# The relative bias of a hybrid decoder step on one core: read from 128 shifted copies in DRAM instead of turned with flip products

## The reference, cut to what matters

```python
b_own = rel_bias[_rel_bucket(q_pos[:, None] - own_pos[None, :])].astype(jnp.float32)
lo = lo + jnp.transpose(b_own, (0, 2, 1))[None]
causal = (own_pos[None, :] <= q_pos[:, None])[None, :, None, :]
lo = jnp.where(causal, lo, NEG)
```

## Time and profile before

| | us |
|---|---|
| median of 3 runs | 1690.98 (1690.12 to 1692.19) |
| the profiled execution's own time | 1688.32 |
| its span, first to last instruction | 1686.6 |
| TensorE busy | 1645.7 (98%) |
| VectorE busy | 1055.3 (63%) |
| ScalarE busy | 616.7 (37%) |
| GpSimd busy | 232.1 (14%) |
| mean granted TensorE clock | 0.992 of 2.4 GHz |

### The profile page before, as it was taken

The page is one execution under the profiler, slowest core; times in us unless marked ns, Lnnn a source line. Parts: engine busy times, 40 slices in busy tenths (PEclk is TensorE's granted clock), DMA queues, the critical chain, the costliest instruction groups (busy, mean ns, idle before and its releaser), DMA issues.

```text
span 1686.6 us, 30879 instructions
## 1 busy us (share of the span) xinstructions
PE 1645.7 (98%) x12884; PEld 1590.6 (94%) x12884; DVE 1055.3 (63%) x1702; ACT 616.7 (37%) x783; POOL 232.1 (14%) x371
## 2 busy tenths in 40 slices
PE   8999999999999999999999999999999999999996
PEld 7998889888898998999999999999999999999996
DVE  5676588455654355586766666666666666666665
ACT  6444323332233334463333333333333333333334
POOL 1112242023202011120101010101010101010004
PEclk9999999899999999999999999999999999999999
DMA  8433345344756565545454545454545454545442
GB/s 248 126 113 112 109 138 151 101 125 129 228 180 193 182 211 170 172 131 157 145 156 144 157 141 159 141 159 140 160 140 161 139 161 139 160 140 158 143 150 82
DMA packets 230171, 255.12 MB, mean 151 GB/s; under 512 B 9036, under 2 KB 220558, under 8 KB 229712
## 3 DMA queue, kind: packets, MB, share of 16 engines
q1 hardware_dynamic: 217488, 220.16, 42.6%
q0 software_dynamic: 9856, 31.71, 6.0%
q10 hardware_dynamic: 2688, 1.27, 0.3%
HBM read 242.00 MB, written 11.12 MB: 150 GB/s over the span
## 4 chain that ended last, share of the span: by engine, by line
PE 87%; DVE 4%; issue 3%; DMA 2%; POOL 2%; ACT 2%; POOLq 0%; DVEq 0%; SPq 0%; ACTq 0%
PE ps_proj L1693 21%; PE ps_proj L1694 20%; PE ps_proj L1695 20%; PE ps_small L1694 6%; PE ps_small L1693 6%; PE ps_small L1695 6%; PE ps_small L1730 2%; ACT w_hi L790 1%; DMA k_pages<-in_cache_k_dram 1%; DMA state_s<-in_state_gdn_dram 1%; DVE w_lo L1127 1%; DVE state_s L1122 1%; PE ps_small L1959 0%; PE ps_small L2070 0%; PE ps_small L1859 0%
## 5 line engine op out<-in xcount | busy, mean ns | idle before, releaser
L1693 PE MATMUL ps_proj<-x_hi,w_hi 128*128 128x320 f32 x2560 | 812.8, 317 | 3.6 <-issue 3.4
L1695 PE MATMUL ps_proj<-x_hi,w_lo 128*128 128x320 f32 x2560 | 794.8, 310 | 0.0
L1694 PE MATMUL ps_proj<-x_lo,w_hi 128*128 128x320 f32 x2560 | 794.8, 310 | 0.0
L1127 DVE TENSOR_TENSOR w_lo<-w_raw,w_hi 128x1024 fp32r<-128x1024 f32 x408 | 500.3, 1226 | 430.2 <-ACT w_hi L790 429.4
L790 ACT ACTIVATE w_hi<-w_raw 128x1024 fp32r<-128x1024 f32 x408 | 431.9, 1059 | 748.0 <-PE ps_proj L1695 551.1
L1693 PEld LDWEIGHTS ps_proj<-x_hi,w_hi 128*128 128x128 f32 x2560 | 483.8, 189 | 19.1 <-issue 15.6
L1694 PEld LDWEIGHTS ps_proj<-x_lo,w_hi 128*128 128x128 f32 x2560 | 484.5, 189 | 1.6 <-issue 1.6
L1695 PEld LDWEIGHTS ps_proj<-x_hi,w_lo 128*128 128x128 f32 x2560 | 484.0, 189 | 0.0
L1693 PE MATMUL ps_small<-hid_hi,w_hi 128*128 128x320 f32 x704 | 217.9, 309 | 0.0
L1695 PE MATMUL ps_small<-hid_hi,w_lo 128*128 128x320 f32 x704 | 217.6, 309 | 0.0
L1694 PE MATMUL ps_small<-hid_lo,w_hi 128*128 128x320 f32 x704 | 217.5, 309 | 0.0
(11 more groups left out here) (329 smaller groups left out, 1078.3 us busy)
## 6 DMA issues: line engine op xcount, KB each, us to landing
w_raw<-in_w_up_dram SPq DMA_DIRECT2D x176, 512.0 KB, 3.5
w_raw<-in_w_in_dram SPq DMA_DIRECT2D x112, 512.0 KB, 3.7
w_raw<-in_w_down_dram SPq DMA_DIRECT2D x88, 512.0 KB, 3.5
w_raw<-in_w_out_dram SPq DMA_DIRECT2D x32, 512.0 KB, 3.7
k_pages<-in_cache_k_dram POOLq DMA_DIRECT2D x32, 256.0 KB, 3.5
v_pages<-in_cache_v_dram POOLq DMA_DIRECT2D x32, 256.0 KB, 4.1
state_s<-in_state_gdn_dram POOLq DMA_DIRECT2D x10, 512.0 KB, 5.6
out_ss_dram<-state_s POOLq DMA_DIRECT2D x8, 512.0 KB, 4.4
```

The costliest lines, as they stand in the source:

```text
L1127: dve.tensor_tensor(wlo[:, slot], raw[:, slot], whi[:, slot].bitcast(F32), ALU.subtract).then_inc(lo_done, 1)
L1693: pe.matmul(o, hi, rhs_hi[:, k0 + kk_, :], start=first and kk_ == 0, stop=False)
L1694: pe.matmul(o, hi, rhs_lo[:, k0 + kk_, :], start=False, stop=False)
L1695: ins = pe.matmul(o, lo, rhs_hi[:, k0 + kk_, :], start=False, stop=last and kk_ == CQ - 1)
```

## The change

The bias row of each head is written 128 times, one behind the other, to a new tensor in DRAM, `rb_copies` (8 x 128 x 384, 1.57 MB), by one transfer from DRAM to DRAM that GpSimd issues in chunk 20. The bias tile is then read with a pitch of 383 entries where a copy is 384 long, so each partition's row begins one entry earlier than the one before: that is the shift in the direction that is wanted. The load goes straight to `bias_q`. The flip products, the copy out of PSUM and the constant `flip` are gone. Since the load now writes `bias_q`, it waits for the last readers of those bytes: in group 0 for `("P", "us", 1, 3)` and the output of the state that lies there, in group 1 for the last SS of group 0. `("G", "hk", 0)` moves from slot (71, 1) to (82, 0), behind the state outputs. The table `LENGTH` loses `hk` of TensorE and gets shorter numbers for the other two, by which the planner puts all steps of group 1 earlier.

```diff
@@ -52,7 +52,6 @@
         "ident": c == r,
-        "flip": c == P - 1 - r,
         "ones": np.ones((P, P)),
@@ -191,7 +190,7 @@
         if k == (1, 2):
-            s += [("P", "gs"), ("A", "gs"), ("G", "gs"), ("G", "hk", 0)]
+            s += [("P", "gs"), ("A", "gs"), ("G", "gs")]
         s += [("P", "kk", *k)]
@@ -254,8 +253,9 @@
 def att_steps(g):
-    s = ([("G", "hk", g)] if g else []) + [("G", "pk", g, 0), ("G", "pk", g, 1)]
-    s += [("P", "hk", g), ("V", "hk", g), ("P", "hb", g), ("V", "hb", g)]
+    s = [("G", "pk", g, 0), ("G", "pk", g, 1)] 
+    s = s + [("G", "hk", g)] if g else [("G", "hk", g)] + s
+    s += [("V", "hk", g), ("P", "hb", g), ("V", "hb", g)]
     for t in range(3):
@@ -301,12 +301,12 @@
           "os": 20, "ot": 6, "gs": 7,
-          "ks": 9, "us": 12, "sh": 11, "hk": 20, "kv": 12, "S": 11, "O": 12, "kt": 10, "hb": 6, "SS": 6, "PT": 4, "PV": 16, "OT": 2, "ab": 76},
+          "ks": 9, "us": 12, "sh": 11, "kv": 12, "S": 11, "O": 12, "kt": 10, "hb": 6, "SS": 6, "PT": 4, "PV": 16, "OT": 2, "ab": 76},
     "A": {"sc2": 25, "sc5": 24, "ab": 10, "qs": 10, "pl": 8, "o": 10, "oq": 0, "kv": 16, "E": 14, "SE": 9, "gs": 10, "kt": 8, "PT": 9, "fp": 22},
     "V": {"sc1": 11, "sc3": 50, "sc4": 15, "ss": 0, "gt": 0, "dm": 10, "dc": 0, "kk": 20, "kq": 9, "tk": 0, "bv": 0,
-          "o2": 0, "oz": 0, "dx": 10, "dh": 4, "df": 4, "dg": 6, "ks": 8, "st": 0, "oc": 10, "o1": 0, "um": 8, "us": 28, "hk": 40,
+          "o2": 0, "oz": 0, "dx": 10, "dh": 4, "df": 4, "dg": 6, "ks": 8, "st": 0, "oc": 10, "o1": 0, "um": 8, "us": 28, "hk": 8,
           "S": 16, "N": 9, "SS": 15, "SN": 7, "kt": 8, "hb": 12, "qz": 3},
-    "G": {"rn": 0, "or": 0, "so": 0, "si": 0, "s2": 0, "gs": 0, "zm": 0, "zv": 0, "kv": 0, "pk": 0, "pv": 0, "hk": 100, "mk": 9, "xd": 0, "qz": 0},
+    "G": {"rn": 0, "or": 0, "so": 0, "si": 0, "s2": 0, "gs": 0, "zm": 0, "zv": 0, "kv": 0, "pk": 0, "pv": 0, "hk": 0, "mk": 9, "xd": 0, "qz": 0},
 }
@@ -338,6 +338,7 @@
     slots[ROOT_AT, 1] += [("P", "root"), ("V", "root")]
+    slots[20, 0].append(("G", "rbcopy"))
     chain = [(x, ROOT_AT + 1) for x in scalar_steps()]
@@ -354,8 +355,6 @@
     def length(x):
-        if x == ("G", "hk", 0):
-            return 0
         return LENGTH[x[0]].get(x[1], 5) * PACE[x[0]] * SPREAD["attention" if x in attention else "delta"]
@@ -397,7 +396,7 @@
 SLOTS = schedule()
-TRANSFERS = {"si", "s2", "so", "gs", "hk", "kv", "pk", "pv"}
+TRANSFERS = {"rbcopy", "si", "s2", "so", "gs", "hk", "kv", "pk", "pv"}
 
@@ -544,7 +543,6 @@
     vp = a.put("v_pages", [P, 4, 2, 4, P])
-    hk = nc.alloc_sbuf_tensor_at("hankel", [P, 4, 2 * P], F32, offset=vp_at + 3 * 4096)
     ob = a.put("o_tok", [P, P])
@@ -569,6 +567,7 @@
     rb_dram = nc.dram_tensor("rb_scratch", (NH, 3 * P), F32, kind="Internal").ap()
+    rb_copies = nc.dram_tensor("rb_copies", (NH, P, 3 * P), F32, kind="Internal").ap()
     psA = nc.alloc_psum_tensor("ps_proj", [P, 4, 512], F32)
@@ -633,7 +632,7 @@
     ab_in, pt_in = sem("ab_in"), sem("page_table_in")
-    rb_out, hk_in, kv_out = sem("rb_out"), sem("hankel_in"), [sem(f"kv_out{i}") for i in range(2)]
+    rb_out, rb_copied, hk_in, kv_out = sem("rb_out"), sem("rb_copied"), sem("hankel_in"), [sem(f"kv_out{i}") for i in range(2)]
     pk_in = [sem(f"k_pages_in{i}") for i in range(2)]
@@ -1433,9 +1432,7 @@
                     g = k[0]
-                    after(dve, "P", "hk", g)
-                    dve.wait_ge(s_out[2], 32)
-                    chain(dve.tensor_copy(bm[:, :, :], psB[:, 2:4, :].rearrange("p k (h x) -> p (k h) x", h=2)))
+                    dve.wait_ge(hk_in, 16 * (g + 1))
                     finish(tt(bm[:, :, P:2 * P], bm[:, :, P:2 * P], over_heads(C("causal"), 4), ALU.add))
@@ -1977,14 +1974,6 @@
 
-                elif name == "hk":
-                    g = k[0]
-                    pe.wait_ge(hk_in, 16 * (g + 1))
-                    after(pe, *(("V", "oz", 1, 2) if g == 0 else ("A", "OT", 0, 1)))
-                    for i in range(2):
-                        ins = pe.matmul(psB[:, 2 + i, :], C("flip"), hk[:, 2 * i:2 * i + 2, :].rearrange("p h x -> p (h x)"),
-                                        start=True, stop=True)
-                    finish(ins)
                 elif name == "kv":
@@ -2021,6 +2010,7 @@
                     after(pe, "V", "hk", g)
+                    after(pe, *(("A", "OT", 0, 1) if g else ("V", "oz", 1, 2)))
                     for h in range(4):
@@ -2298,15 +2288,20 @@
                         pool.dma_start(gs_[r * P - rows_p:r * P - rows_p + n, :], gst[0:n, r, :]).then_inc(gs_out, 16)
+                elif name == "rbcopy":
+                    pool.wait_ge(rb_out, 16)
+                    pool.dma_start(rb_copies, rb_dram.unsqueeze(1).broadcast_to([NH, P, 3 * P])).then_inc(rb_copied, 16)
                 elif name == "hk":
...
                     if g == 0:
-                        pool.wait_ge(rb_out, 16)
-                        after(pool, "A", "gs")
+                        pool.wait_ge(rb_copied, 16)
+                        pool.wait_ge(s_out[2], 32)
+                        after(pool, "P", "us", 1, 3)
                     else:
-                        after(pool, "P", "PV", 0, 1)
-                    src = bass.AP(rb_dram.tensor, 4 * g * 3 * P, [[1, P], [3 * P, 4], [1, 2 * P]])
-                    pool.dma_start(hk[:, :, :], src).then_inc(hk_in, 16)
+                        after(pool, "P", "SS", 0, DB - 1)
+
+                    src = bass.AP(rb_copies.tensor, 4 * g * P * 3 * P + P - 1, [[3 * P - 1, P], [P * 3 * P, 4], [1, 2 * P]])
+                    pool.dma_start(bm[:, :, :], src).then_inc(hk_in, 16)
                 elif name == "kv":
@@ -2329,8 +2324,6 @@
                             after(pool, "P", "PV", *((g, 0) if b > 3 else (0, 1)))
-                        if b == 3:
-                            after(pool, "P", "hk", g)
                         cache, tile_, arrived = I["cache_v"], vp, pv_in
```

## The result

| | before | the change |
|---|---|---|
| median of 22 runs, us | 1689.16 (1684.27 to 1692.95) | 1692.03 (1689.77 to 1698.13) |
| ratio | | 1.0021, interval 1.0012 to 1.0031 |
| the profiled execution, us | 1688.32 | 1692.54 |
| its span, us | 1686.6 | 1690.8 |
| mean granted clock in it | 0.992 | 0.991 |

The change makes the kernel slower by 0.21%, 3.5 us, with an interval of 2.0 to 5.2 us. The ratio is not the quotient of the two medians, which differ by 2.9 us. The profiled executions differ by 4.2 us.

A forecast was written before the change was run, and what follows sets the result against it. TensorE, busy 98%, was taken to bound the kernel. Terms -3.4 + 2.8 + 2.9 + 1.6 + 0 = +3.9 us, added to the median 1690.98, gave 1694.9 us, slower by 0.23%; range 1690.4 to 1698.0.

The forecast's parts named there:

- Removed: Flip products of both groups on TensorE go, 1.71 us a group: -3.4 us.
- The gap of group 0: TensorE waits at `P hb`, near chunk 82, for VectorE's mask, which waits for the bias load: +2.8 us, 2.4 to 3.6.
- The gap of group 1: TensorE waits at `P hb`, chunk 113, for the mask, which follows `x_lo` on VectorE: +2.9 us, 2.7 to 3.1.
- The clock: TensorE's granted clock falls behind one of the two new gaps, one chance in two each: +1.6 us, 0 to 3.2.
- my rival of 1696.5 us: The clock falls behind both new gaps at `P hb`: +5.5 us in all, chance 0.15.
- What was put at nothing: Copy in chunk 20, later group 0 pages and V steps, group 1 running earlier: 0 us.
- The copy: GpSimd issues the 1.57 MB transfer in chunk 20, 0.89 us inside an idle time of 1.48 us: 0 us.
- The earlier place of group 1: Group 1 runs 4 to 5 chunks earlier with the same distances between steps: 0, within 1 us either way.
- The traffic: Rival: transfers in chunk 20 and around 550 make one weight chunk 3.5 us late: +7.4, 1698.4 us, chance 0.05.
- A missing gap: Rival: no wait at one `P hb` and no fall of the clock: -0.5, 1690.5 us, chance 0.08.
- The faster rival: Low-clock stretches before the changed steps run at full clock, giving back 5.8 us: -3.5, 1687.5 us, chance 0.07.
- the slow stretches of the linear part: Lower granted clock for 12 us from 320 and 4 us at 272, costing 4.6 and 1.2 us, 5.8 in all.

The follow-up runs named there:

- the kernel with the flips twice: The kernel before, with each pair of flip products issued twice into the same banks: ratio 1.0020, 1693.2 us.
- the versions without gaps: The change with planned lengths altered so that both `P hb` come later, group 1 three chunks early or all steps in old slots: 0.9974, again 0.9988; 0.9967.
- the old data path with the new table: The kernel before, keeping flip products, PSUM copy and small load, with only the planner's `hk` lengths as in the change: ratio 1.0025, 1692.5 us.
- both late: The change with `P hb` planned in a later slot in both groups, (83, 1) and (114, 2): ratio 0.9974, run again 0.9988.
- the copy alone: The kernel before, plus the 1.57 MB transfer in chunk 20, which nothing reads; first `hankel` load waits for it: ratio 0.9977, run again 1.0004.
- group 1 late: The change with only group 1's `P hb` planned later, at (114, 2), group 0's as in the change: ratio 1.0003, 1687.7 us.
- gaps filled: The change with three unread products of constants on TensorE ahead of each wait for the mask: ratio 1.0013, 1691.0 us.

## Why the prediction was right, point by point

The forecast was +3.9 us, slower by 0.23%; measured was 0.21%, 3.5 us by the ratio and 2.9 by the medians. Both gaps came where they were put and for the reason given. That the sum came so close owes something to luck, in the term for the clock. The absolute figure, 1694.9, was 2.9 us above the median of 22 runs. Most of that is the starting point: the three runs shown had a median of 1690.98, and 22 runs of the same kernel have 1689.16.

**Removed, -3.4 us.** Right: 1.72 us a pair by the kernel with the flips twice.

**The gap of group 0, +2.8 (2.4 to 3.6).** Right in kind, 0.5 us too small: 3.3. The term that was mis-sized is the load. I took 5.6 us to landing, between the earlier trace rows; it took 6.3, near rows 7, the ones nearest in surroundings. That is 0.7 us more, and TensorE started 0.05 us behind the mask, not 0.14. In group 1 the load landed 7.1 us after its issue, directly behind four page loads. Whether the layout of the source, rows of 1 KB from 128 places, or only the traffic makes it slower than the 4.3 and 5.1 us of `hankel` was not tried. By the Trainium skill (DMA: Bandwidth & Descriptors, Anatomy of one DMA) the estimate for it is 3.2 us, half of what was measured under this traffic; by that estimate VectorE alone would have set the gap.

**The gap of group 1, +2.9 (2.7 to 3.1).** Right: 2.7, from the order on VectorE alone.

**The clock, +1.6 (0 to 3.2).** The weak term. I took one chance in two for each gap, so one fall. In both profiles of the change the clock fell behind both new gaps, and it fell behind all seven waits for the mask of 2.28 us or more in the five profiles that have them unfilled. The net count of the first profile was one more all the same, since the old fall at chunk 112 was missing there; in the second profile, an execution of 1695.5 us, it was not. With two falls for certain the sum would have been +5.5, my rival of 1696.5 us, outside the measured interval. Over all runs the change was granted 0.9910 and the kernel before about 0.9921 (98 runs beside the experiments). Within those 98 runs the time goes with the clock:

| mean granted clock of a run | runs | mean time, us |
|---|---|---|
| 0.989 | 2 | 1692.4 |
| 0.990 | 16 | 1691.1 |
| 0.991 | 20 | 1689.9 |
| 0.992 | 19 | 1688.3 |
| 0.993 | 17 | 1686.7 |
| 0.994 | 20 | 1685.9 |
| 0.995 | 4 | 1684.0 |

A line through all 98 gives 1.4 us for 0.001 (1.0, 1.4 and 1.7 on the three chips). At that rate the lower clock would be 1.5 us of the 3.5. But the versions without gaps were granted 0.9910 and 0.9914 too, and the old data path with the new table 0.9915 where the kernel before had 0.9916, so I can't put this share down to the gaps. The size agrees, the cause stays open. That the same wait of 2.99 us is followed by a fall in one execution and not in the next agrees with the rule of the Trainium skill (TensorE: Matmul & The Clock Gate, Part 1: The HAM clock gate) that the watch does not start with the kernel.

**What was put at nothing.** The copy: confirmed, though its issue took 1.18 us and not 0.89. The earlier place of group 1: waits for key pages rose from 1.8 to 2.7 us, those for `v_tok` fell by 0.5, inside the 1 us that I allowed. The 1.8 is itself unsteady: a second profile of the kernel before has 0.6, and the second one of the change has 3.6. Between these two the rise is 3.0 us, more than I allowed.

**The sum with the waits that were measured,** for the first two profiled executions: -3.4 + 3.3 + 2.7 + 0.9 - 0.5 gives +3.0, and with one fall at the price that I took, 1.6, +4.6, against 4.2.

**The rivals.** The traffic is excluded by both late and by the copy alone. A missing gap: both were there. The faster rival needed the slow stretches of the linear part to go. In the profile of the change they stand; but in four of the 14 profiles the one at 320 us was missing (the first of the copy alone, the second of both late, group 1 late, and the old data path with the new table), so such a stretch can go for an execution. My ground against it, that three runs agreed within 2.1 us, was weak: 22 runs of the same kernel spread over 8.7 us.

## What to carry to other kernels

When a step is replaced by a cheaper one, read what its length did for the others. The old numbers in the planner's table, 40 for the copy and, in group 1, 100 for the load, were wrong as durations of the new work, but they kept TensorE's next step behind VectorE's queue; with true durations the planner sent TensorE to a result that VectorE, held by work ahead in its own order, could not have ready. The gain was there all the time, 3.4 us by the removed products, and setting one length per group brought it out: 4.4 and 2.0 us by the two ratios, the second with an interval that ends at 1.0000. On a kernel in which one engine is 98% busy, a removed operation pays only if nothing the engine then reaches sooner makes it wait: check, at the new place, when the releaser can finish by its own program order.

## What the runs showed of the hardware that I had not expected

The kernel before, unchanged, took between 1682.25 and 1693.94 us in 98 runs, and the mean granted clock of a run, 0.989 to 0.995, goes with it at 1.4 us for 0.001. Differences of 0.2% came with the clock here for one and the same kernel: a comparison of 10 runs with 28 gave 0.9977 with an interval up to 0.9990 for an edit that gave 1.0004 when it was run again.

A wait of 3.0 us in the same place, with the same instructions around it, was followed by a fall of the clock to 1.2 GHz in the profile of the kernel before and by none in the first one of the change. Of the 14 profiles, 11 have that fall and 3 do not. The length of a wait alone does not tell which: a wait of 2.45 us for `v_tok` (group 1 late) was followed by none, one of 2.00 us (gaps filled) by a fall.
